# A hybrid attention and DeltaNet block: other buffer addresses, an early copy of the input, a read-back on another queue, and stages moved

## The reference

```python
h = x + rmsnorm(token_mixer(rmsnorm(x, ln_mix_pre)), ln_mix_post)
y = h + rmsnorm(conv_ffn(rmsnorm(h, ln_ffn_pre)), ln_ffn_post)
```

## Time and profile before

| | |
|---|---|
| median of 3 runs | 1279.46 us |
| profiled execution | 1280.17 us |
| its span, first to last instruction | 1278.3 us |
| mean granted clock of TensorE | 0.992 |
| chunks of weights | 204 of 1 MB |
| matmuls L1306, L1308 | 2048 each |
| matmuls L1322, L1323, L1324 | 608 each |

### The profile page before, as it was taken

One profiled execution on the slowest core, in us unless ns is written; L12 is line 12 of the kernel. 1 busy time (PEld: TensorE's weight loads), 2 busy tenths in 40 slices (PEclk: granted clock), 3 DMA queues, 4 the chain that ended last, 5 costly groups with the idle time before them and its releaser, 6 DMA issues.

```text
span 1278.3 us, 20109 instructions
## 1 busy us (share of the span) xinstructions
PE 1239.3 (97%) x6635; PEld 1062.1 (83%) x6635; DVE 885.5 (69%) x1627; ACT 736.0 (58%) x1449; POOL 220.9 (17%) x258
## 2 busy tenths in 40 slices
PE   7899899999999999899999999999999999999996
PEld 5788798889887888788888888888888888888885
DVE  6678966785454655688878887887888874554544
ACT  5786546744677654576566556656655554444442
POOL 1122220232022000022222312222231210000000
PEclk9999999999999999899999999999999999999998
DMA  9455533562333555265455455555555565555541
GB/s 378 150 213 133 199 112 120 148 251 99 137 132 129 197 197 191 78 226 192 169 197 195 166 197 189 185 185 193 185 179 197 175 234 183 197 192 177 191 165 66
DMA packets 33029, 226.81 MB, mean 177 GB/s; under 512 B 4160, under 2 KB 4816, under 8 KB 6352
## 3 DMA queue, kind: packets, MB, share of 16 engines
q1 hardware_dynamic: 31536, 221.40, 49.0%
q10 hardware_dynamic: 1440, 4.71, 1.0%
HBM read 223.86 MB, written 2.24 MB: 177 GB/s over the span
## 4 chain that ended last, share of the span: by engine, by line
PE 86%; DVE 5%; ACT 4%; DMA 3%; issue 1%; POOL 0%; SPq 0%; DVEq 0%; ACTq 0%; POOLq 0%
PE bank L1306 32%; PE bank L1308 16%; PE bank L1324 11%; PE bank L1323 11%; PE bank L1322 11%; DVE w_lo L871 2%; DVE arena L892 1%; DMA raw<-in_wts 1%; DMA xfeat<-in_x 1%; DMA xfeat<-in_x_tok 1%; PE bank L1420 1%; ACT w_hi L463 1%; PE bank L1396 1%; PE bank L1413 1%; PE bank L1411 1%
## 5 line engine op out<-in xcount | busy, mean ns | idle before, releaser
L871 DVE TENSOR_TENSOR w_lo<-raw,w_hi 128x512 fp32r<-128x512 f32 x816 | 570.1, 720 | 279.4 <-ACT w_hi L463 275.5
L1306 PE MATMUL bank<-xhl,w_hi 128*128 128x512 f32 x2048 | 731.8, 398 | 11.9 <-DVE w_lo L871 9.4
L463 ACT ACTIVATE w_hi<-raw 128x512 fp32r<-128x512 f32 x816 | 502.3, 630 | 375.6 <-PE bank L1324 190.2
L1308 PE MATMUL bank<-xhl,w_lo 128*128 128x256 f32 x2048 | 581.4, 284 | 0.0
L1306 PEld LDWEIGHTS bank<-xhl,w_hi 128*128 128x128 f32 x2048 | 387.8, 189 | 101.2 <-issue 9.7
L1308 PEld LDWEIGHTS bank<-xhl,w_lo 128*128 128x128 f32 x2048 | 388.1, 190 | 0.2
L1322 PE MATMUL bank<-w_hi,ffn_act 128*128 128x512 f32 x352 | 138.9, 395 | 0.0
L1323 PE MATMUL bank<-w_lo,ffn_act 128*128 128x512 f32 x352 | 138.9, 395 | 0.0
L1324 PE MATMUL bank<-w_hi,ffn_act 128*128 128x512 f32 x352 | 138.9, 395 | 0.0
L435 POOL TENSOR_TENSOR arena<-arena,token_scale 128x256 f32<-128x256 f32 x88 | 78.0, 900 | 308.4 <-DVE arena L876 192.7
L1228 DVE SCALAR_TENSOR_TENSOR arena<-arena,fcw 128x256 f32<-128x256 f32 x176 | 85.3, 485 | 23.9 <-DVE arena L1228 1.5
(11 more groups left out here) (220 smaller groups left out, 976.0 us busy)
## 6 DMA issues: line engine op xcount, KB each, us to landing
raw<-in_wts SPq DMA_DIRECT2D x204, 1024.0 KB, 4.8
xfeat<-in_x SPq DMA_DIRECT2D x4, 512.0 KB, 9.2
xfeat<-in_x_tok ACTq DMA_DIRECT2D x1, 2048.0 KB, 12.8
arena<-base_rows SPq DMA_DIRECT2D x4, 512.0 KB
out_y<-xfeat SPq DMA_DIRECT2D x4, 512.0 KB, 2.9
arena<-gate_rows SPq DMA_DIRECT2D x1, 1024.0 KB, 4.2
arena<-in_post_gains ACTq DMA_DIRECT2D x1, 1024.0 KB, 6.4
down_gain<-in_post_gains ACTq DMA_DIRECT2D x1, 1024.0 KB, 4.7
```

The source lines that it names most:

```text
L463: nc.scalar.activation(w_hi[:, i % RING, :], raw[:, slot, quarter * PIECE:(quarter + 1) * PIECE], ACT.Copy).then_inc(hi_ready, 1)
L871: V.tensor_tensor(w_lo[:, i % RING, :], raw[:, slot, quarter * PIECE:(quarter + 1) * PIECE], w_hi[:, i % RING, :].bitcast(f32), ALU.subtra ...
L1306: M(ps[j][:, :], w_hi[:, r % RING, w], xhl[:, k, :, :].rearrange("p a t -> p (a t)"), start=(k == 0), stop=False, skip_group_check=True)
L1308: last = M(ps[j][:, 0:T], w_lo[:, r % RING, w], xhl[:, k, 0, :], start=False, stop=(k == KT - 1), skip_group_check=True)
```

## The change

Nine edits:

- The large buffers `xfeat`, `raw`, `w_hi`, `w_lo` are declared after the small ones, behind a pad (56 words) that ends at a multiple of 512 bytes. They begin at bytes 9728, 26112, 58880 and 75264, `xhl` at 91648, the arena at 124416: all multiples of 512. The arena has 48 words less.
- A second load of `x` in token form, `xcopy`, goes into the arena (over `tmat` to the first quarter head of `dm`, all unused then). ScalarE issues it after its split of piece 5. The squares read it, behind places 7 and 9; their output `xsq` moves to other tiles, and the root stands behind place 11.
- The load into `res` goes to SyncE's queue, behind place 10.
- `ba_sum` stands behind place 14 on VectorE, before the copies of the scale (`scale`, 15). The scale's matmul is at 14, before the turn of `ba` (16). Gates at 21, `gcum` 24, `grow` 27.
- The Silu of the first group stands at 10 instead of 11, its convolutions at 3, 5, 7, 9.
- DeltaNet: `qt` +15, `vt` +19, `spread` +39, `turn` +41, `x`, `y` and all later stages +2; the second batch begins at 115.
- SyncE only writes the packed blocks. ScalarE waits for them and issues the read-back at +14.
- Attention: from 186, the second batch 19 places later, at 205.
- TensorE: 14 matmuls (128x512 of `xhl` into bank 0, which nobody reads) before the first `hidden_t`, behind `m_evac` 1.

In the diff, `sp` is SyncE, `act_e` ScalarE, `dve` VectorE and `pe` TensorE.

```diff
-SILU_AT = [11, 9, 10, 15, 15, 15]
-CONV_AT = [(4, 6, 8, 9)] + [(1, 3, 5, 7)] * 2 + [(1, 5, 9, 13)] * 3
+SILU_AT = [10, 9, 10, 15, 15, 15]
+CONV_AT = [(3, 5, 7, 9)] + [(1, 3, 5, 7)] * 2 + [(1, 5, 9, 13)] * 3
-PLACE = {"ba": 9, "ba_turn": 16, "stat": 18, "gate": 22, "gcum": 26, "grow": 28}
-for _b, _l in enumerate((44, 114)):
+PLACE = {"ba": 9, "stat": 14, "ba_turn": 16, "scale": 15, "gate": 21, "gcum": 24, "grow": 27}
+for _b, _l in enumerate((44, 115)):
-        PLACE["qt", _b, _g] = _l + 12 + _g
-        PLACE["vt", _b, _g] = _l + 15 + _g
-        PLACE["spread", _b, _g] = _l + 38
-        PLACE["turn", _b, _g] = _l + 39 + _g
+        PLACE["qt", _b, _g] = _l + 15 + _g
+        PLACE["vt", _b, _g] = _l + 19 + _g
+        PLACE["spread", _b, _g] = _l + 39
+        PLACE["turn", _b, _g] = _l + 41 + _g
+    PLACE["load", _b] = _l + 14
-        PLACE["x", 2 * LEVELS * _b + _i] = _l + 41 + 9 * _i // 4
-        PLACE["y", 2 * LEVELS * _b + _i] = _l + 44 + 9 * _i // 4
-    for _name, _n in (("z0", 57), ("s", 59), ("o0", 59), ("ks", 61), ("qs", 61), ("z1", 63), ("o1", 65), ("rs", 67)):
+        PLACE["x", 2 * LEVELS * _b + _i] = _l + 43 + 9 * _i // 4
+        PLACE["y", 2 * LEVELS * _b + _i] = _l + 46 + 9 * _i // 4
+    for _name, _n in (("z0", 59), ("s", 61), ("o0", 61), ("ks", 63), ("qs", 63), ("z1", 65), ("o1", 67), ("rs", 69)):
-SB_PLACE = 183
+SB_PLACE = 186
-    _s = SB_PLACE + 20 * _r
+    _s = SB_PLACE + 19 * _r
...
+        line = 512
+        pad = sb("pad", [P, (-nc.sbuf_base) % line // 4])
+        xfeat = sb("xfeat", [P, KT, T])
...
-        xsq = arena[:, a0:a0 + D]
-        xdiag = arena[:, a0 + D:a0 + D + T].rearrange("p (j c) -> p j c", j=NJ)
+        xsq = arena[:, 40 * T:40 * T + D]
+        xdiag = arena[:, a0:a0 + T].rearrange("p (j c) -> p j c", j=NJ)
+        xcopy = arena[:, a0 + T:a0 + T + NJ * D].rearrange("p (j d) -> p j d", j=NJ)
...
+            follow(10)
+            sp.wait_ge(s("xn_lo"), KT)
+            sp.dma_start(res, x_tok).then_inc(s("x_tok_in"), 16)
...
                 sp.dma_start(scratch[b], packed.rearrange("p u i -> p (u i)")).then_inc(s("scratch_in"), 16)
-                sp.wait_ge(s("scratch_in"), 16 * (b + 1))
-                for jh in range(2):
...
             split(0, 5)
+            act_e.dma_start(xcopy, x_tok).then_inc(s("x_copy_in"), 16)
             input_hi(2)
...
-            act_e.wait_ge(s("xn_lo"), KT)
-            act_e.dma_start(res, x_tok).then_inc(s("x_tok_in"), 16)
...
-            follow(12)
-            act_e.wait_ge(s("x_tok_in"), 16)
+            follow(7)
+            act_e.wait_ge(s("x_copy_in"), 16)
...
-                follow(12 + j)
-                nc.scalar.activation(xsq, res[:, j, :], ACT.Square, accum_out=stat[:, 3, j:j + 1]).then_inc(s("x_sq"), 1)
+                follow(7 + 2 * j)
+                nc.scalar.activation(xsq, xcopy[:, j, :], ACT.Square, accum_out=stat[:, 3, j:j + 1]).then_inc(s("x_sq"), 1)
+            follow(11)
...
-            follow(PLACE["stat"] + 2)
+            follow(PLACE["ba_turn"] + 2)
...
+                follow(PLACE["load", b])
+                act_e.wait_ge(s("scratch_in"), 16 * (b + 1))
+                for jh in range(2):
...
-            follow(12)
+            follow(10)
             dve.wait_ge(s("x_sq"), NJ)
...
-            follow(14)
+            follow(12)
             dve.wait_ge(s("row_root"), 1)
...
+            follow(14)
             dve.wait_ge(s("ba_mm"), 1)
...
-            follow(PLACE["stat"])
+            follow(PLACE["scale"])
             dve.wait_ge(s("x_sum"), 1)
...
+            follow(PLACE["ba_turn"] + 1)
             dve.wait_ge(s("gate_in"), 16)
...
+            follow(PLACE["stat"])
+            pe.wait_ge(s("const_ready"), 1)
+            pe.wait_ge(s("x_diag"), NJ)
+            M(ps[4][:, 0:T], ones[:, :], xdiag.rearrange("p j c -> p (j c)"), start=True, stop=True).then_inc(s("x_sum"), 1)
             follow(PLACE["ba_turn"])
             pe.wait_ge(s("ba_sum"), 1)
...
-            follow(PLACE["stat"])
-            pe.wait_ge(s("const_ready"), 1)
-            pe.wait_ge(s("x_diag"), NJ)
-            M(ps[4][:, 0:T], ones[:, :], xdiag.rearrange("p j c -> p (j c)"), start=True, stop=True).then_inc(s("x_sum"), 1)
...
+            pe.wait_ge(s("m_evac"), 1)
+            for _ in range(14):
+                M(ps[0][:, :], xhl[:, 1, 0, 0:P], xhl[:, 0, :, :].rearrange("p a t -> p (a t)"), start=True, stop=True)
             hidden_t(0)
```

More of the change, by code:

```diff
@@ L109, in sem @@
             return ctx.enter_context(nc.semaphore(name))
-        xfeat = sb("xfeat", [P, KT, T])
-        res = xfeat[:, :, :].rearrange("p k t -> p (k t)").rearrange("p (j d) -> p j d", j=NJ)
-        raw = sb("raw", [P, RAW, CHUNK])
-        w_hi = sb("w_hi", [P, RING, PIECE], f32r)
-        w_lo = sb("w_lo", [P, RING, PIECE], f32r)
         half = sb("half", [P, 4, T])
@@ L128, in hybrid_block_kernel @@
         token_scale = sb("token_scale", [P, 2, T])
+        line = 512
+        pad = sb("pad", [P, (-nc.sbuf_base) % line // 4])
+        xfeat = sb("xfeat", [P, KT, T])
+        res = xfeat[:, :, :].rearrange("p k t -> p (k t)").rearrange("p (j d) -> p j d", j=NJ)
+        raw = sb("raw", [P, RAW, CHUNK])
+        w_hi = sb("w_hi", [P, RING, PIECE], f32r)
+        w_lo = sb("w_lo", [P, RING, PIECE], f32r)
         halfs = [half[:, i, :] for i in range(4)]
```

10 lines of the change are left out of this document (5 added, 5 removed).

## The result

| | median, us | lowest to highest | runs |
|---|---|---|---|
| before | 1280.37 | 1276.64 to 1283.54 | 4 |
| after | 1267.77 | 1259.02 to 1269.24 | 4 |

The ratio is 0.9888 (95% interval 0.9857 to 0.992), 1.1% faster; the medians lie 12.6 us or 1.0% apart. The median is 1.3 us above the 1266.5 predicted. The profiled execution of after took 1266.38 us, its span is 1264.5. The number came out nearly right and its terms did not. Most lines named here stand 8 to 10 higher in the new kernel: L871 is L879, L1306 is L1316, L1308 is L1318, L1322 to L1324 are L1332 to L1334, L1514 is L1524, L1600 is L1610. L1375 is L1380.

The account below looks back on a forecast made before the run. TensorE was taken to bound the kernel, idle for 39 us of 1278.3, with half-clock stretches behind waits. The terms summed to 12.9 us off 1280.2: 1267.3 profiled, 1266.5 as a median, range 1246 to 1277.

Parts of the forecast that it names:

- Alignment: Starts of w_hi and xhl moved to multiples of 512 bytes: no change in matmul pace, 0 us; upper bound 92 us.
- rival 1: All matmuls: the pace rises with the alignment; 1236 us for a third of the excess, 1174 for all; chance 0.15.
- The third rival: All matmuls: moving and stationary operands now start alike and the pace falls; 35 us lost, 1301 us; chance 0.06.
- Early copy: Start, first norm: the wait at L1361 and its half clock go, x's last quarter comes later; +3.3 us, bounds -2 to +5.1.
- Gates: Gate stages: the 1.9 us wait at L1375 for ke_arg goes; +1.9 us, bounds 0 and +1.9.
- vt and qt: DeltaNet: vt moves behind the Silu, so the 2.0 us wait at L1380 goes; +2.0 us, bounds 1.0 and 2.0.
- Read-back and turn: Base blocks: chunk 18 no longer late, TensorE's waits and half clock near 155 go; +5.7 us, bounds 2.5 and 5.7.
- Attention: Attention batches: one more table load for the Silu ahead of L1514; -1.0 us second batch, -0.5 first; bounds +1 and -4.
- 14 matmuls: Output norm: added matmuls fill TensorE's 3.8 us idle time and keep the clock up; +1.5 us, bounds 0 and 2.2.
- What I wrote would prove me wrong: Sign for the changed profile: the pair of a 128x512 and a 128x256 matmul takes anything but 0.35 us.
- the other sign: Sign of being wrong in the changed profile: TensorE's waits stand elsewhere with the same sum.

Follow-up runs that it names:

- e1: After with the large buffers back at the old addresses (192 and 320 bytes past a multiple of 512), so the new schedule alone: 1276.75 us, ratio 0.9982.
- the four edits: Changes to after: early copy on SyncE's queue, group 12's Silu behind the logarithms, last two z turns later, first DeltaNet batch's levels one place later: 1250.92 us.
- e12: e11 put back on the old addresses (w_hi 192, xhl 320 bytes past a multiple of 512): 1265.42 us, ratio 0.9895.
- e11: After with the four edits, on after's addresses: 1250.92 us, ratio 0.9775.
- e2: Before with nothing changed but the addresses, which are those of after: 1263.52 us, ratio 0.9871.
- e7: e1 with the Silu of token group 12 moved from place 208 to 210, behind the second attention batch's logarithms: 1272.37 us, ratio 0.9959.
- e8: e1 with the read-back of the base blocks issued on SyncE right behind the store again, as in before: 1281.67 us, ratio 1.0021.
- e10: e1 without the 14 added matmuls ahead of the output norm's transposes and their wait for m_evac: 1277.84 us in one execution.
- e9: e1 with the early copy issued on SyncE behind its first eight loads, plus a ScalarE wait for small_in: 1272.01 us, ratio 0.9937.
- e3: Before with w_hi and w_lo at multiples of 512 bytes, xhl and the arena 64 past one: 1286.92 us in one execution.
- e5: Before with xhl and the arena at multiples of 512 bytes, w_hi and w_lo still 192 past one: 1280.58 us in one execution.
- e4: Before with all large buffers 128 bytes past a multiple of 512: 1276.63 us in one execution.
- e13: e11 with all buffers 128 bytes past a multiple of 512: 1260.44 us.

## Why the prediction was right, and where it was wrong

**Alignment: taken as 0, measured 9 to 16 us, in favour.** This step failed. By the medians the addresses gave 9.0 us on the new schedule (e1 to after), 14.5 with the four edits (e12 to e11) and 16.0 on the old schedule (before to e2). I had bounds up to 92 us and chose 0 from two rows. The runs took a tenth to a sixth of these 92 us; rival 1 was given 0.15 and set at a third. The rule I quoted from the Trainium skill, "SBUF — State Buffer", Specifications, that the memory has 16-byte lines, would have made these starts alike; the runs disagree. The estimate by the N / 2.4 GHz + 2.5 ns of the Trainium skill's "TensorE: Matmul & The Clock Gate", "Wait — 56ns, not 53.3ns?", stays far off even when aligned: 226.7 ns against 215.8 for 512 columns. The third rival's sum mixes two counts: its 3872 counts a pair as one, its excess of 15 ns counts each matmul, and per pair or single the excess is 92 us / 3872 = 24 ns.

**Early copy: +3.3 taken, about -1.4 in after, near my lower bound, and +0.7 in e1.** (The first stretch of the table, 7.7 us before, less the 1.2 us that the gates' wait puts into it in the new order.) The wait at L1361 did go, with the half clock at 42. I had let the two queues share the DMA engines as the old copy did, 160 of 410 GB/s, and put the quarter 2.8 us late (my own 6.4 less 4 make 2.4); it was 4.6 late. I saw the mechanism and its bound, and took the middle. I missed that a wait of 3 us here can bring a slow stretch of its own, at 26 us: it did in after, e1 and e7, not in e8 and e10. The Trainium skill, "DMA: Bandwidth & Descriptors", section on queues, rings and completion order, says that each DMA engine takes turns between the queues it has work for; by that an even share was to be expected. My estimate by it: 1.6 MB at 205 instead of 410 GB/s come 3.9 us later, and the measured 4.6 us agree better with that. With the copy in the one queue (e9) the start loses 2.1 us instead of 7.7: a little more than my whole upper bound of 5.1.

**Gates: +1.9 taken.** The wait of 1.9 us at L1375 has become one of 1.0 us (1.1 in e1) at L1380 for L982 near 56 us: about +0.8, inside its bounds.

**vt and qt: +2.0, right.** The wait is gone and none has followed; the second stretch of the table, 4.0 us with the gates' 1.9 in it, goes to 0.8 in after and to nothing in e1.

**Read-back and turn: +5.7 taken, +4.7 in e1, 2.7 in after.** The mechanism was right: e8 gives back 3.9 of them. What came next I had not named: rows finished sooner do not help the levels. VectorE is behind by then, as its timeline in after shows, while GpSimd spreads (the second block):

```profile
148.57 4.36 DVE L900 SCALAR_TENSOR_TENSOR arena<-arena,dcw 128x255 f32<-128x255 f32 x3
152.85 4.70 DVE L879 TENSOR_TENSOR w_lo<-raw,w_hi 128x512 fp32r<-128x512 f32 x4
157.47 1.51 DVE L900 SCALAR_TENSOR_TENSOR arena<-arena,dcw 128x255 f32<-128x255 f32 x3
```

```profile
148.06 3.16 POOL L400 TENSOR_TENSOR arena<-arena 128x512 f32<-128x512 f32 x2
151.19 2.89 POOL L358 TENSOR_TENSOR arena<-arena 128x512 f32<-128x512 f32 x2
```

Three operations that take 1.51 us take 4.36 beside GpSimd's. Before had the same (4.32 us at 152). TensorE then waits 2.0 us at L1406, and in after the clock falls once more. (The list of waits names no engine for this wait, so that VectorE's delay makes it is argued.) The Trainium skill, "SBUF — State Buffer", on the two sides of SBUF, says that VectorE with two inputs in SBUF and a GpSimd operation that reads SBUF lock each other out; the rows agree.

**Attention: -1.5 taken, -5.8 in e1, -8.5 in after.** This step failed by its size and lies beyond its bound of -4. The named cause, one more table load ahead of the logarithms, was right; the price was not. The Silu puts its own work as well as two table loads ahead of the logarithms, the wait of 4.6 us brings a slow stretch of 6.9 us (3.4 lost), and in after the z turn's wait of 2.0 us brings one more of 3.5.

**14 matmuls: +1.5, right** (33.6 us to 32.1 for the stretch), as was the clock of 1.00 from 520 to 527.

**The sum.** The schedule was to give 12.9 us. Alone it gave 2 to 4 (e1: 2.8 by the medians, 3.9 by the spans). My terms up to 240 us came to 12.9 (the last two cancel) and the trace shows 8.5 of it in e1 (7.7 + 4.0 + 6.9 against 8.2 - 0.3 + 2.2); the attention stages took most of that back. That 1266.5 lay 1.3 us from the median is chance: I left out the 9.0 us of the addresses on this schedule and counted 10.1 us too much for the schedule (12.9 less e1's 2.8). Which pattern of the pair an execution falls into is worth as much again, and after's four executions lie on both sides of the forecast. What I wrote would prove me wrong did: "if the pair of matmuls takes anything but 0.35 us". At the two digits of a timeline it still reads 0.35 (0.3466 or 0.3534); the windows of 400 us show it. So did the other sign, "if these waits stand elsewhere with the same sum": outside the start and the output norm they make 15.3 us before and 14.1 after.

## What to carry to other kernels

Put both operands of an fp32r matmul at multiples of 512 bytes: 128 are enough for single 128x512 matmuls here, but the fast pattern of the pair was seen to last through the up stage at 512 only. Check the pace by counting matmuls in a long window without waits, since differences of 2% don't show in single rows. When a prediction rests on two rows that agree, ask whether they differ at all in the thing that is changed. A schedule change is worth its waits plus the clock stretches behind them, and a moved stage must be costed with everything that it is moved past: the queue it now shares, the table it evicts, the engine it runs beside.

## What the runs showed of the hardware that I had not expected

- A matmul of 512 columns costs 226.7 ns with both operands at multiples of 128 bytes, 232.4 with both 64 bytes off, and 233.3 with one of them off (e3, e5). So aligning one operand alone makes it slower, by 0.9 ns.
- A pair of 512 and 256 columns has two steady paces when aligned, 346.6 and 353.4 ns, kept for hundreds of microseconds. In the up stage it has one with the old starts, 351.1, and with one operand aligned 348.9 (`xhl`, e5) or 353.3 (`w_hi`, e3). So aligned code can also be slower (the up stage of e2, e4 and e13).
- Misaligned matmuls aren't always slow. Of the 14 added ones, both operands of which lie in `xhl`, 64 bytes off in e1, the first nine distances between starts are 224 to 238 ns and the last four 226 or 227; in e9 all from the fourth on are 226 or 227, and in after all thirteen. Why stays open.
- The same wait may bring down the clock or not. The 2.0 us at L1406 are followed by half clock in after, e7, e9 and e10 and not in e1; the z turn's 1.6 to 2.1 us in after and e8, and not in e1, e7, e9 and e10. Each costs 1.7 us more when it does. The 2.4 to 3.3 us at L1316 near 25 us are followed by it in after, e1 and e7 (3.4 to 6.8 us of it), not in e8 and e10.
